# Sample cross-attention of a hybrid decoder step, issued four samples at a time in column groups of the array

## The chip, the cores and the metric

The kernel runs on one core of a Trainium2 chip. The metric is the device time of one execution in microseconds (us). A core has a matrix engine (TensorE, "PE" in the profile, with its weight loads "PEld"), a vector engine (DVE), a scalar engine (ACT), GpSimd (POOL) and a queue engine (SP). They run their own instruction streams and meet at semaphores. Transfers from main memory are issued by SP (weights) and POOL (cached keys and values).

## The reference

One inference step of a two-layer decoder for one prompt of 512 tokens and 8 samples of 4 new tokens each. Both groups share all weights. Every layer is a token mixer, a cross-attention into 256 memory tokens and a SwiGLU block. The change touches the cross-attention of the samples only, in both layers:

```python
def cross_attend(h, mk, mv, wq, wo):
    b, t, _ = h.shape
    q = (h @ wq).reshape(b, t, XATTN_HEADS, XATTN_HEAD_DIM)     # 4 heads of 256
    o, _ = gqa_attend(q, mk, mv, True)
    return o.reshape(b, t, D_MODEL) @ wo
...
        xs = xs + rmsnorm(cross_attend(rmsnorm(xs, gn[2]), cache_mem_k[li], cache_mem_v[li], w_xq[li], w_xo[li]), gn[3])
```

For each sample and head the scores are a 4 x 256 by 256 x 256 product, followed by a softmax over the 256 memory tokens and a 4 x 256 by 256 x 256 product with the values. Each sample has its own keys (1 MB) and its own values (1 MB) per layer, so 32 MB are read for this in all. All of it is float32.

## The kernel before

Activations stand with the channels on the 128 partitions: `x`, `h`, `y` and `mix` hold 8 chunks of 128 channels by 544 tokens (512 of the prompt, then 32 of the samples). `layer_end(l)` runs for both layers: output projection, memory projections, `linear("xq")`, `cross(l)`, `linear("xo")`, and the feed-forward block.

`cross(l)` on TensorE has, in the order of the program:

- `scores(0)`: scores of the first 128 prompt tokens (16 records of 256 columns in the trace, 8 instructions in the program; a float32 matmul leaves two records).
- The scores of the samples. Sample b has its 4 tokens x 4 heads in 16 of 32 columns of a weight tile `xqd[:, b, c, :]`; samples 2q and 2q+1 share the 32 output partitions 32q to 32q+31 of one PSUM bank (the even one fills the first 16, and the other columns are zero). Eight channel chunks c are added up, with the key tile `mk` as the moving operand, 256 columns. The loop is over b, and c is inside.
- `scores(1)`, `turn(0)` (transposes of prompt probabilities), two transposes of the samples' probabilities, then `s_values(0)`: values of samples 0 to 3. Sample j writes output partitions 32j to 32j+31 of two banks f, 512 columns each, adding up two halves kt of the memory tokens. The loop is over j, with f and kt inside.
- `scores(2)`, `turn(1)`, `s_turn(0)`, `scores(3)`, `turn(2)`, `s_values(1)` for samples 4 to 7, `turn(3)`, `s_turn(1)`, and `values()` for the prompt.

Output partitions 32j to 32j+31 belong to columns 32j to 32j+31 of the array. These 32-column strips are called column groups here.

ACT and DVE work between: for each prompt quarter `x_exp` on ACT takes the exponentials and `x_soft` on DVE the maxima and the scaling; `x_evac` on ACT copies the transposes; `s_copy(hb)` copies the value rows of four samples, one bank on each of the two engines, once the count `mv_used` says that the four samples are done.

Key and value tiles of 1 MB come through a ring of 6 places. `TILES` is the order in which POOL loads them; `PLACE` says where tile n goes (n mod 6 here, counted from the layer's first key tile), and `BEFORE` which tile was there. POOL works through the list in order and, ahead of each load, waits until the place's last tile has been used: `mk_used` counts used key tiles and `mv_used` used value tiles. With 8 key tiles and 8 value tiles per layer, key tiles 0 to 5 of the list are loaded well ahead. Key tile 6 takes the place of key tile 0, 7 that of 1, value tile 0 that of key tile 2, value tile 1 that of key tile 3, value tiles 2 and 3 those of key tiles 4 and 5, value tiles 4 and 5 those of key tiles 6 and 7, and value tiles 6 and 7 those of value tiles 0 and 1:

```python
            def tile(n):
                kind, b, kv, hh = TILES[n]
                s = PLACE[n]
                if BEFORE[n] is not None:
                    tile_used(BEFORE[n])
                ...
                else:
                    pool.dma_start(dst, a["mem" + kv][int(kind[3]), b]).then_inc(cfull[s], 16)
```

TensorE waits in `tile_in` for the place's `cache_full` semaphore. The sparse attention earlier in the kernel (L1588 with `to_rows`, `k_scores`, `s_first`) already issues its 32-column matmuls in turn over the four column groups.

Of the kernel before, what the change touches and what calls it, by code (L numbers as in the profile page):

```python
# [34 lines left out]
P = 128  # L35
# [3 lines left out]
NB, NT = 8, 4  # L39
# [125 lines left out]
TILES = [("cmp", b, kv, h) for b in range(NB) for kv in "kv" for h in range(2)]  # L165
for _hb in range(2):
# [4 lines left out]
    if not _hb:  # L171
        TILES += [("win", 1, "k", 0)]
    TILES += [("slc", 4 * _hb + j, "v", h) for h in range(2) for j in range(4)]
TILES += [("mem0", b, kv, 0) for kv in "kv" for b in range(NB)]
TILES += [("mem1", b, kv, 0) for kv in "kv" for b in range(NB)]
TILE = {t: i for i, t in enumerate(TILES)}

XC = 2
# [80 lines left out]
def decoder_step(nc, a, w, o):  # L259

    with ExitStack() as ctx:
# [13 lines left out]
        def S(name):  # L275

            if name not in sems:
                sems[name] = ctx.enter_context(nc.semaphore(name))
            return sems[name]
# [25 lines left out]
        ps = ctx.enter_context(nc.psum_tensor("ps", [P, 8, 512], F32))  # L305
# [66 lines left out]
        xqd = flatx[:, 1280:3328].rearrange("p (b c n) -> p b c n", b=NB, c=8)  # L372
# [69 lines left out]
        def tile_in(e, *t):  # L442

            n = TILE[t]
            e.wait_ge(cfull[PLACE[n]], 16 * TURN[n])
            return place_of(n)
# [71 lines left out]
        def _(pool):  # L518
# [6 lines left out]
            def tile_used(n):  # L525

                kind, b, kv, hh = TILES[n]
                if kind == "cmp":
                    pool.wait_ge(S("sub_ready"), n + 1)
                elif kind == "win":  # L530
                    pool.wait_ge(S("sw_sc" if kv == "k" else "sw_pv"), b + 1)
                elif kind == "slc" and kv == "k":
                    pool.wait_ge(S("kt_tr"), 32 * (b // 4) + 4 * (4 * hh + 3) + b % 4 + 1)
                elif kind == "slc":
                    pool.wait_ge(S("sv_used"), 8 * (b // 4) + 4 * hh + b % 4 + 1)
                else:
                    pool.wait_ge(S("mk_used" if kv == "k" else "mv_used"), 8 * int(kind[3]) + b + 1)

            def tile(n):
                kind, b, kv, hh = TILES[n]  # L540
# [37 lines left out]
            k = 0  # L578
            at = NC
# [1004 lines left out]
        def _(pe):  # L1584
            pe.wait_ge(S("const_loaded"), 32)

            def mm(out, lhsT, rhs, start, stop, **kw):
                return pe.matmul(out, lhsT, rhs, start=start, stop=stop, **kw)  # L1588
# [128 lines left out]
            for u in range(32):  # L1717
                c, g, qt = u // 8, u // 4 % 2, u % 4
# [205 lines left out]
            def cross(l):  # L1924
# [35 lines left out]

                def s_values(hb):

                    for j in range(4):
                        b = 4 * hb + j
                        mv = tile_in(pe, f"mem{l}", b, "v", 0)
                        for f in range(2):
                            for kt in range(2):
                                at = kt * P + 32 * (b // 2)
                                last = mm(ps[32 * j:32 * j + 32, 6 * hb + f, :], xst[:, at:at + 32],
                                          mv[:, kt * 1024 + 512 * f:kt * 1024 + 512 * f + 512], kt == 0, kt == 1)  # L1970
                        last.then_inc(S("mv_used"), 1)

                def s_turn(hb):
                    pe.wait_ge(S("xv_copied_a"), 2 * l + hb + 1)
# [6 lines left out]
                scores(0)  # L1981

                pe.wait_ge(S("xq_apart"), l + 1)
                for b in range(NB):
                    mk = tile_in(pe, f"mem{l}", b, "k", 0)
                    rows = slice(32 * (b // 2), 32 * (b // 2) + 32)
                    for c in range(8):
                        last = mm(ps[rows, 1, 0:256], xqd[:, b, c, :], mk[:, c * 256:c * 256 + 256],
                                  b % 2 == 0 and c == 0, b % 2 == 1 and c == 7)
                    last.then_inc(S("mk_used"), 1)  # L1990
                scores(1)
                turn(0)
                pe.wait_ge(S("xs_norm"), l + 1)
# [195 lines left out]
```

## Time and profile before

| what | value |
|---|---|
| median of 3 runs | 2095.23 us (2095.05 to 2095.54) |
| the profiled execution | 2096.04 us, span 2094.1 us from first to last instruction |
| TensorE busy | 1894.8 us, 90% of the span |
| DVE, ACT, POOL busy | 1001.5, 694.8, 255.8 us |
| memory read | 244.89 MB, 123 GB/s over the span |
| mean granted TensorE clock | 0.954 of full speed |

Nearly all matmuls are recorded on L1588, the helper `mm`; they are told apart by the tiles that they read. In the trace `mc` is the buffer with the ring's places, `big` holds queries and probabilities, `kstore` and `vstore` the prompt's keys and values. `cross(0)` runs from about 636 to 718 us of the span and `cross(1)` from about 1514 to 1598 us. Matmul durations include the way through the array, so that one can start before the one ahead ends; the distance between starts is what a matmul costs.

### The profile page before, as it was taken

The page shows a single profiled execution, that of the slowest core. Times are in us where ns is not written, and L with a number is a line of the kernel's source. Part 1 is how long each engine was busy: PE and PEld are TensorE (multiplying, and loading weights), DVE is VectorE, ACT ScalarE, POOL GpSimd, SP SyncE. Part 2 cuts the span into 40 slices and gives each one's busy share as a digit, 9 for nine tenths or more (in the row PEclk, how much of TensorE's full clock was granted, in tenths as well). Part 3 has the DMA queues.
Part 4 walks back from the last instruction along what each step waited for, and adds up shares of the span by engine and source line. Part 5 has one row for each costly group of instructions (what it writes and reads, how often), then busy time and mean ns, then how long its engine had stood idle before and what let it go on. Part 6 is the DMA issues. An engine that isn't in the chain of part 4 may idle for free.

```text
span 2094.1 us, 31811 instructions
## 1 busy us (share of the span) xinstructions
PE 1894.8 (90%) x13423; PEld 1690.5 (81%) x13423; DVE 1001.5 (48%) x1405; ACT 694.8 (33%) x1155; POOL 255.8 (12%) x231
## 2 busy tenths in 40 slices
PE   5997997669899989999999899798999799999995
PEld 4785664449795679999999799797946799999995
DVE  6994784333642246444422394738322554444223
ACT  2113553344421433222222326545214432222221
POOL 2330001212221021000000112114010300000001
PEclk9997998889999989999999899999999899999998
DMA  6894004762445122222222222335450122222221
GB/s 218 343 372 171 1 1 178 274 268 96 148 164 199 36 67 71 90 82 88 90 84 89 75 71 83 107 137 168 144 201 31 51 91 82 89 90 84 88 85 59
DMA packets 59655, 254.73 MB, mean 122 GB/s; under 512 B 10224, under 2 KB 10624, under 8 KB 45904
## 3 DMA queue, kind: packets, MB, share of 16 engines
q1 hardware_dynamic: 40320, 135.39, 20.1%
q0 software_dynamic: 14656, 109.53, 13.6%
q10 hardware_dynamic: 4576, 8.34, 1.1%
q8 instruction: 77, 1.26, 0.2%
q14 instruction: 26, 0.21, 0.0%
HBM read 244.89 MB, written 12.68 MB: 123 GB/s over the span
## 4 chain that ended last, share of the span: by engine, by line
PE 79%; DVE 12%; ACT 4%; DMA 3%; issue 1%; POOL 0%; SPq 0%; ACTq 0%; POOLq 0%; DVEq 0%
PE ps L1588 75%; DVE work L1107 3%; PE ps L1839 2%; DVE big L1168 1%; PE ps L1756 1%; DVE work_r L1129 1%; DVE rinv L1091 1%; DVE wring_r L1121 1%; ACT whi L679 1%; DMA mc<-in_slck,idx 1%; DVE x L1110 1%; DMA big<-in_slck,idx 1%; ACT work L852 1%; DVE mc L1549 0%; DMA cst<-in_const 0%
## 5 line engine op out<-in xcount | busy, mean ns | idle before, releaser
L1588 PE MATMUL ps<-work_r,whi 128*128 128x272 f32 x4352 | 762.2, 292 | 49.4 <-ACT work_r L691 27.5
L1588 PEld LDWEIGHTS ps<-work_r,whi 128*128 128x128 f32 x4352 | 633.6, 191 | 63.5 <-issue 42.2
L1588 PE MATMUL ps<-work_r,wring_r 128*128 128x272 f32 x2432 | 512.1, 293 | 0.0
L679 ACT ACTIVATE whi<-wring 128x1024 fp32r<-128x1024 f32 (+1 forms) x232 | 242.3, 1045 | 793.2 <-PE ps L1588 791.1
L1121 DVE TENSOR_TENSOR wring_r<-wring,whi 128x1024 fp32r<-128x1024 f32 (+1 forms) x232 | 283.4, 1224 | 439.6 <-ACT whi L679 439.3
L1588 PEld LDWEIGHTS ps<-work_r,wring_r 128*128 128x128 f32 x2432 | 388.6, 193 | 0.0
L1588 PE MATMUL ps<-mc_r,whi 128*128 128x272 f32 x1216 | 242.5, 289 | 0.0
L1588 PE MATMUL ps<-big_r,whi 128*128 128x272 f32 (+1 forms) x960 | 198.1, 293 | 14.0 <-DVE wring_r L1121 14.0
L1588 PEld LDWEIGHTS ps<-mc_r,whi 128*128 128x128 f32 x1216 | 188.5, 189 | 0.0
L1588 PEld LDWEIGHTS ps<-big_r,whi 128*128 128x128 f32 x960 | 155.3, 195 | 15.3 <-DVE wring_r L1121 15.2
L1588 PE MATMUL ps<-mc_r,wring_r 128*128 128x272 f32 x704 | 145.7, 288 | 0.0
L1588 PE MATMUL ps<-work,wring 128*128 128x272 f32 x480 | 119.0, 409 | 6.7 <-DVE work L1098 6.7
L1168 DVE TENSOR_REDUCE big<-mc 128x128 f32<-128x2048 f32 x32 | 115.6, 3680 | 9.7 <-DMA mc<-in_cmpk,idx 7.6
L1588 PEld LDWEIGHTS ps<-work,wring 128*128 128x128 f32 x480 | 95.2, 200 | 27.8 <-issue 7.4
L571 POOL TENSOR_TENSOR ssum<-ssum,sq 128x544 f32<-128x544 f32 (+1 forms) x56 | 78.9, 1409 | 262.7 <-ACT sq L656 260.8
L571 POOL TENSOR_TENSOR ssum<-sq 128x544 f32<-128x544 f32 (+1 forms) x13 | 17.5, 1349 | 758.2 <-ACT sq L656 758.2
L1588 PEld LDWEIGHTS ps<-mc_r,wring_r 128*128 128x128 f32 x704 | 109.9, 189 | 0.0
L1466 DVE TENSOR_TENSOR kstore<-ps,rinv 128x544 f32<-128x544 f32 x44 | 31.9, 724 | 151.1 <-PE ps L1588 151.1
L1588 PE MATMUL ps<-mc,big 128*32 128x256 f32 (+2 forms) x448 | 89.9, 432 | 5.3 <-ACT big L918 5.3
L1461 DVE TENSOR_TENSOR big<-ps,rinv 128x544 f32 (+1 forms) x44 | 31.9, 724 | 112.1 <-PE ps L1588 112.0
L1588 PEld LDWEIGHTS ps<-mc,big 128*32 128x32 f32 x448 | 37.5, 111 | 54.3 <-issue 24.7
L1091 DVE RECIPROCAL rinv<-rms 128x544 f32<-128x544 f32 (+1 forms) x14 | 46.1, 3295 | 27.9 <-ACT rms L668 27.9
(296 smaller groups left out, 2062.8 us busy)
## 6 DMA issues: line engine op xcount, KB each, us to landing
wring<-w_ffn SPq DMA_DIRECT2D x88, 512.0 KB, 3.5
mc<-in_memk POOLq DMA_DIRECT2D x16, 1024.0 KB, 7.5
mc<-in_memv POOLq DMA_DIRECT2D x16, 1024.0 KB, 5.1
wring<-w_down SPq DMA_DIRECT2D x32, 512.0 KB, 3.5
wring<-w_w_out SPq DMA_DIRECT2D x16, 512.0 KB, 4.0
wring<-w_mk SPq DMA_DIRECT2D x16, 512.0 KB, 3.4
wring<-w_mv SPq DMA_DIRECT2D x16, 512.0 KB, 4.1
wring<-w_xq SPq DMA_DIRECT2D x16, 512.0 KB, 3.6
```

The source lines that it names most:

```text
L571: pool.tensor_tensor(ssum[:, 0:wd], sq[:, 0, 0:wd] if c == 1 else ssum[:, 0:wd], sq[:, c % 2, 0:wd], ALU.add).then_inc(S("sq_summed"), 1)
L679: act.activation(dst, src, ACT.Copy).then_inc(S("w_hi"), 1)
L852: act.activation(piece, piece, ACT.Exp, bias=sst[:, 3 * hb + 2, 1:2], scale=SC, accum_out=sxs[:, k:k + 1]).then_inc(S("sx_exp"), 1)
L1091: dve.reciprocal(rinv[:, 0:wd], rms[:, 0:wd]).then_inc(S("rinv_ready"), 1)
L1107: dve.tensor_tensor(y[:, c, :], y[:, c, :], rinv[:, :], ALU.mult).then_inc(S("y_scaled"), 1)
L1110: dve.tensor_tensor(x[:, c - 1, :], x[:, c - 1, :], y[:, c - 1, :], ALU.add).then_inc(S("x_ready1"), 1)
L1121: dve.tensor_tensor(lo, src, F(hi), ALU.subtract).then_inc(S("w_lo"), 1)
L1168: dve.tensor_reduce(subs[:, n % 8, :], src.rearrange("p (r c) -> p c r", r=SUB), AXX, ALU.add).then_inc(S("sub_ready"), 1)
L1461: dve.tensor_tensor(halves(hid[j]), accp[g % 4], halves(rinv[:, :]), ALU.mult).then_inc(drained[g % 4], 1)
L1466: dve.tensor_tensor(halves(uprow[:, j, :]), accp[g % 4], halves(rinv[:, :]), ALU.mult).then_inc(drained[g % 4], 1)
L1588: return pe.matmul(out, lhsT, rhs, start=start, stop=stop, **kw)
L1839: last = pe.transpose(ps[:, j, r * P:r * P + P], kt_[:, at:at + P], ident)
```

## The change

The samples' matmuls of both products are put in another order, and the key tiles are loaded in the order in which they are now used. The matmuls themselves, their number, operands and output places stay the same.

- Scores: first the even samples 0, 2, 4, 6 (`e = 0`), then the odd ones (`e = 1`). Inside each, the loop over chunks c is outside, and the four samples, each in its own column group, follow one another. All four key tiles are waited for ahead of the first matmul, and the four counts of `mk_used` come with the last round, c = 7.
- Values: bank f and half kt are outside, and the four samples follow one another. All four tiles are waited for first, and the four counts of `mv_used` come with the last round.
- `TILES`: key tiles in the order 0, 2, 4, 6, 1, 3, 5, 7 (`MEMK`), and POOL's wait follows it.

```diff
-TILES += [("mem0", b, kv, 0) for kv in "kv" for b in range(NB)]
-TILES += [("mem1", b, kv, 0) for kv in "kv" for b in range(NB)]
+
+MEMK = [2 * q + e for e in range(2) for q in range(4)]
+for _l in range(2):
+    TILES += [(f"mem{_l}", b, "k", 0) for b in MEMK]
+    TILES += [(f"mem{_l}", b, "v", 0) for b in range(NB)]
...
-                    pool.wait_ge(S("mk_used" if kv == "k" else "mv_used"), 8 * int(kind[3]) + b + 1)
+                    at_ = MEMK.index(b) if kv == "k" else b
+                    pool.wait_ge(S("mk_used" if kv == "k" else "mv_used"), 8 * int(kind[3]) + at_ + 1)
...
-                    for j in range(4):
-                        b = 4 * hb + j
-                        mv = tile_in(pe, f"mem{l}", b, "v", 0)
-                        for f in range(2):
-                            for kt in range(2):
-                                at = kt * P + 32 * (b // 2)
+                    mvs = [tile_in(pe, f"mem{l}", 4 * hb + j, "v", 0) for j in range(4)]
+                    for f in range(2):
+                        for kt in range(2):
+                            for j in range(4):
+                                at = kt * P + 32 * ((4 * hb + j) // 2)
                                 last = mm(ps[32 * j:32 * j + 32, 6 * hb + f, :], xst[:, at:at + 32],
-                                          mv[:, kt * 1024 + 512 * f:kt * 1024 + 512 * f + 512], kt == 0, kt == 1)
-                        last.then_inc(S("mv_used"), 1)
+                                          mvs[j][:, kt * 1024 + 512 * f:kt * 1024 + 512 * f + 512], kt == 0, kt == 1)
+                                if f and kt:
+                                    last.then_inc(S("mv_used"), 1)
...
-                for b in range(NB):
-                    mk = tile_in(pe, f"mem{l}", b, "k", 0)
-                    rows = slice(32 * (b // 2), 32 * (b // 2) + 32)
+                for e in range(2):
+                    mks = [tile_in(pe, f"mem{l}", 2 * q + e, "k", 0) for q in range(4)]
                     for c in range(8):
-                        last = mm(ps[rows, 1, 0:256], xqd[:, b, c, :], mk[:, c * 256:c * 256 + 256],
-                                  b % 2 == 0 and c == 0, b % 2 == 1 and c == 7)
-                    last.then_inc(S("mk_used"), 1)
+                        for q in range(4):
+                            last = mm(ps[32 * q:32 * q + 32, 1, 0:256], xqd[:, 2 * q + e, c, :],
+                                      mks[q][:, c * 256:c * 256 + 256], e == 0 and c == 0, e == 1 and c == 7)
+                            if c == 7:
+                                last.then_inc(S("mk_used"), 1)
```

On TensorE, the scores of the samples in `cross(0)` stood so before (`cache_full0` to `cache_full5` are the ring's places, in brackets what an instruction waits for):

```order
L1588 MATMUL ps<-mc,big 32x256 [waits cache_full0,xq_apart]
L1588 MATMUL ps<-mc,big 32x256 x7
L1588 MATMUL ps<-mc,big 32x256 [waits cache_full1]
L1588 MATMUL ps<-mc,big 32x256 x7
...
L1588 MATMUL ps<-mc,big 32x256 [waits cache_full0]
L1588 MATMUL ps<-mc,big 32x256 x7
L1588 MATMUL ps<-mc,big 32x256 [waits cache_full1]
L1588 MATMUL ps<-mc,big 32x256 x7
L1588 MATMUL ps<-kstore,big 128x256 [waits xp_exp]
```

And so they stand now:

```order
L1592 MATMUL ps<-mc,big 32x256 [waits cache_full2,cache_full1,cache_full3,cache_full0,xq_apart]
L1592 MATMUL ps<-mc,big 32x256 x31
L1592 MATMUL ps<-mc,big 32x256 [waits cache_full0,cache_full1,cache_full5,cache_full4]
L1592 MATMUL ps<-mc,big 32x256 x31
L1592 MATMUL ps<-kstore,big 128x256 [waits xp_exp]
```

The second filling of places 0 and 1 was waited for ahead of the seventh and the eighth sample, after 48 and 56 of the 64 matmuls; now both are waited for together after 32 of them.

The first values, `s_values(0)`, on TensorE in `cross(0)` before:

```order
L1588 MATMUL ps<-mc,big 32x512 [waits cache_full2,xs_trc]
L1588 MATMUL ps<-mc,big 32x512 x3
L1588 MATMUL ps<-mc,big 32x512 [waits cache_full3]
L1588 MATMUL ps<-mc,big 32x512 x3
L1588 MATMUL ps<-mc,big 32x512 [waits cache_full4]
L1588 MATMUL ps<-mc,big 32x512 x3
L1588 MATMUL ps<-mc,big 32x512 [waits cache_full5]
L1588 MATMUL ps<-mc,big 32x512 x3
```

And now:

```order
L1592 MATMUL ps<-mc,big 32x512 [waits cache_full4,cache_full3,cache_full5,cache_full2,xs_trc]
L1592 MATMUL ps<-mc,big 32x512 x15
```

The tiles in places 3 to 5 were waited for one after another, between matmuls; now all four are waited for at the start. POOL's list of loads has the same length and the same waits by name.

## Rows read from the trace of the kernel before

**Rows 1.** The page: the chain that ended last, share of the span by engine.
```profile
PE 79%; DVE 12%; ACT 4%; DMA 3%; issue 1%; POOL 0%; SPq 0%; ACTq 0%; POOLq 0%; DVEq 0%
```

**Rows 2.** Chain of work that ended last in cross(0): start, us, what.
```profile
639.88 28.89 PE ps L1588 x144
...
672.53 12.51 PE ps L1588 x48
```

**Rows 3.** Timeline of PE, cross(0): start, us, operation, records [idle before <-releaser].
```profile
639.81 25.31 PE L1588 MATMUL ps<-mc,big 128*32 128x256 f32 x128
665.05 3.72 PE L1588 MATMUL ps<-kstore,big 128*128 128x256 f32 x16
...
672.53 8.86 PE L1588 MATMUL ps<-mc,big 128*32 128x512 f32 x32 [2.67 <-ACT big L918]
681.32 3.72 PE L1588 MATMUL ps<-kstore,big 128*128 128x256 f32 x16
...
693.06 8.86 PE L1588 MATMUL ps<-mc,big 128*32 128x512 f32 x32
```

**Rows 4.** Timeline of PE, the same places in cross(1).
```profile
1518.21 25.31 PE L1588 MATMUL ps<-mc,big 128*32 128x256 f32 x128
...
1550.93 10.53 PE L1588 MATMUL ps<-mc,big 128*32 128x512 f32 x32 [2.67 <-ACT big L918]
1561.39 3.72 PE L1588 MATMUL ps<-kstore,big 128*128 128x256 f32 x16
```

**Rows 5.** Timeline of weight loads: in the first scores, then in s_values(0).
```profile
640.26 3.56 PEld L1588 LDWEIGHTS ps<-mc,big 128*32 128x32 f32 x17
...
673.42 0.11 PEld L1588 LDWEIGHTS ps<-mc,big 128*32 128x32 f32 x1 [0.32 <-issue]
673.85 0.11 PEld L1588 LDWEIGHTS ps<-mc,big 128*32 128x32 f32 x1 [0.32 <-issue]
```

**Rows 6.** Timeline of PE in the sparse attention, matmuls in turn over column groups.
```profile
374.07 0.64 PE L1588 MATMUL ps<-kstore,small 128*32 128x256 f32 x8
374.52 1.04 PE L1588 MATMUL ps<-big,small 128*32 128x512 f32 x8
375.38 0.27 PE L1588 MATMUL ps<-big,work 128*32 128x128 f32 x1
...
378.77 0.27 PE L1588 MATMUL ps<-big,work 128*32 128x128 f32 x1
```

**Rows 7.** Timeline of POOL: first key load of cross(0), and four loads in a row.
```profile
643.75 0.53 POOL L553 DMA_DIRECT2D mc<-in_memk  x1 [54.80 <-PE ps L1588]
...
1354.81 2.18 POOL L553 DMA_DIRECT2D mc<-in_memk  x4 [65.39 <-DVE mc L1563]
```

**Rows 8.** Landing times (us from issue): at 643.7, 1522.1, 1355.4 (second of four), 588.4.
```profile
mc<-in_memk POOLq DMA_DIRECT2D x1, 1024.0 KB, 6.4
mc<-in_memk POOLq DMA_DIRECT2D x1, 1024.0 KB, 5.0
mc<-in_memk POOLq DMA_DIRECT2D x1, 1024.0 KB, 7.1
mc<-in_memk POOLq DMA_DIRECT2D x1, 1024.0 KB, 9.7
```

**Rows 9.** An idle stretch of PE in the timeline; then stretches: us, PE busy (records), granted clock, DMA share, GB/s.
```profile
388.09 0.39 PE L1588 MATMUL ps<-mc,work 128*32 128x128 f32 x1 [8.39 <-DMA mc<-in_slcv,idx]
...
187.00:213.00 26.00, 16.43 (x43) 0.50 0.00 1
388.00:391.00 3.00, 2.91 (x56) 0.50 1.02 429
391.50:393.00 1.50, 1.50 (x64) 1.00 0.28 109
1551.80:1555.00 3.20, 3.20 (x7) 0.50 0.00 0
```

**Rows 10.** Timeline of DVE: scaling of the last prompt quarter's probabilities.
```profile
695.93 1.22 DVE L1415 TENSOR_TENSOR big<-big,small 128x1024 f32<-128x1024 f32 x1
```

## The prediction

> **What bounds the kernel now.** I read four views. The page first: the chain of work that ended last is 79% TensorE [rows 1], so time taken from TensorE is time taken from the kernel wherever nothing else is late. Then that chain in the stretch around the first cross-attention: it goes through the samples' scores without a break (28.89 us over 144 records: 16 of the prompt's and the samples' 128) and, after a step over ACT, through the samples' values [rows 2]. Then the timeline of TensorE for the lengths. The scores run from 639.81 to 665.05, 25.24 us. The values of samples 0 to 3 run from 672.53 to 681.32, 8.79 us [rows 3], and in the second layer from 1550.93 to 1561.39, 10.46 us [rows 4]; the values of samples 4 to 7 are the same 32 records and 8.86 us long [rows 3]. The scores of the second layer have the same 25.31 us [rows 4]. So the reordered matmuls hold TensorE for 25.2 + 8.8 + 8.8 and 25.2 + 10.5 + 8.8 us, 87.3 us in both layers.
>
> **What one matmul costs alone and in turn.** Seventeen weight loads, one for each record, take 3.56 us in the first sample's scores, so the starts are (3.56 - 0.11) / 16 = 0.216 us apart for 256 columns; in the values they are 0.43 us apart for 512 [rows 5]. The sparse attention shows 32-column matmuls that go round the four column groups, with the same types and widths: eight records of 256 columns take 374.52 - 374.07 = 0.45 us, eight of 512 take 0.86 us, and 31 rounds of four records of 128 columns take 378.77 - 375.38 = 3.39 us, 0.109 us for a round [rows 6]. A round of four costs what one record costs alone. I take that: the rotation is worth a factor of four. The Trainium skill (TensorE: Matmul & The Clock Gate, "Why this matters for your kernels") gives 2.38 for three column groups and 3.07 for four row groups, 512 columns each. The trace has a duration for the same thing, and it says 4.0; by 3.07 the sum below would come out about 7 us later.
>
> **Scores, part by part.** The even samples are 64 records, 16 rounds of 0.216 us: 3.46 us. Their four key tiles were loaded long before. Then the program wants four tiles at once for the odd samples, and two of them (samples 5 and 7, places 0 and 1) can't be issued before the even ones are done. This is the new wait. POOL issued its first key load of the stage 643.75 - (639.81 + 3.46) = 0.48 us after the first sample's last record [rows 3, 7]; now the four counts come together at the same 3.46 us, so the issue stays at start + 3.94. The next issue follows 0.55 us later (four in 2.18 us) and the second load of a row landed 7.1 us after its own issue, 7.65 after the first's [rows 7, 8]. A single load took 5.0 us in the second layer and 6.4 in the first [rows 8]; the second comes some 2.6 us behind. So the last tile is there at start + 3.94 + 7.7 = 11.6 us (second layer) and, with the 1.4 us that the first layer's load was longer, some 1.2 us later, 12.8. TensorE idles for about 8 us. Behind it nothing can go: the engine is in order, and scores(1), turn(0) and the values are queued behind the odd samples. The other loads (values 0 and 1) are issued behind the two and don't hold them up.
>
> The odd samples are another 3.46 us at full clock. After the idle 8.39 us at 388.09 the granted clock was 0.50 from before the restart until past 391, and 1.00 by 391.5 [rows 9]. Some 3.4 us at the half level cost 1.7 us: 5.2 us. The scores end at start + 16.8 (layer 1) and + 18.0 (layer 0) instead of + 25.24: a gain of 8.4 + 7.2 = **15.6 us**.
>
> **Wait for values.** From the end of the scores to the first values it is 672.53 - 665.05 = 7.48 us, set by prompt work and ACT's exponentials [rows 3]. That stays. Value tiles 2 and 3 go to the places of key tiles 4 and 5, which are now freed only at the end of the scores. Issued some 0.4 us later, the second lands 7.7 us after that, at 8.1: a wait of 0.6 us in each layer, **-1.2 us**. Tiles 0 and 1 were issued 8 us before, and samples 4 to 7 have 681.32 to 693.06 = 11.7 us for tiles 6 and 7 against 8.1 needed.
>
> **First values.** 8 rounds of 0.43 us: 3.43 us. The idle time ahead of them (2.67 us now) grows to 3.3; after 2.67 us the clock was 1.00 in one layer and 0.50 for 3.2 us in the other [rows 3, 4, 9]. I charge half of that loss, 0.85 us: 4.3 us against 8.79 and 10.46, **10.7 us** gained.
>
> **Second values.** 3.43 us instead of 8.79, but now something else is late. The next instruction on TensorE, turn(3), wants the scaled probabilities of the last prompt quarter, and DVE has them at 695.93 + 1.22 = 697.15, 4.09 us after the values start [rows 3, 10]. So turn(3) starts at + 4.13 instead of + 8.79: 4.66 us in each layer, **9.3 us**. ACT and DVE copy the value rows within 0.7 us of the count, beside turn(3). Copies and prompt values keep their distances.
>
> The other edits cost nothing: POOL issues the same 16 loads per layer, and loading the keys in another order moves bytes but adds none; number and length of weight loads stay. The cover for the loads of keys 5 and 7 was the scores of samples 2 to 5; that cover is gone, and it is priced above.
>
> **Sum.** 15.6 - 1.2 + 10.7 + 9.3 = 34.4 us. From the profiled execution's own 2096.04 us that is 2061.6; the median of the runs is 0.8 us lower, so 2061 us.
>
> **Bounds of the unknown.** The wait for the second key tile: 7.7 us as in an idle queue, or 0.55 + 9.7 = 10.3 us as for two loads that shared the engines with weights [rows 8]; I stay with the first, since no weights are due here. It is worth +4 us over both layers, and the slower first load of layer 0 -1.2. The clock in the odd samples: full, -3.4 us, or half all through (6.9 us), +3.5. The clock in the first values: full -1.7, half all through +5.2. The wait for values: none -1.2. The forecast's own range is thus 2053 to 2069.
>
> **Rivals.**
>
> *Each burst is cold* (20%). The waits fall between short bursts, and the half level might hold from the first idle stretch through all of them. For: the trace has 26 us at 0.50 with 16.43 us of work in it [rows 9], and TensorE would now work some 10 us of the 21 after the even samples. Against: in the sparse attention one restart was enough. Price per layer: 1.7 us in the odd samples are in the sum already; scores(1) and the turns, about 4 us, double, of which 0.6 covers the wait for values: 3.4. The first values take 6.9 instead of 4.3: 2.6. The second take 6.9 instead of 4.13: 2.8. Together 8.8, about 18 in both layers: 2079 us; with the bursts alone cold, 2072. The Trainium skill has this as a rule against such a change (same page, "HAM oscillation — how this bites in real kernels"): short bursts with load waits between them start cold each time. The trace shows it for the burst right behind a long wait.
>
> *The rotation pays less* (5%), because four different key tiles stream at once. Against: in rows 6 four different tiles streamed as well. At a factor of two the even and the odd samples cost 3.46 us more each, the first values 3.43 and the second 6.86 - 4.13 = 2.7: 13 per layer, 2087 us. With no factor at all nothing is gained and the wait is left, so this is also the way in which the change would not do what it says.
>
> *The wait is shorter than I think* (7%). Without any idle time between even and odd samples (8 us and 1.7 us of clock, twice) the time would be 2042 us. Against: a 1 MB tile never landed in under 5.0 us here, and the place must be free first.
>
> *Slower than before* (3%). One mechanism: the long wait takes the clock to the half level and it doesn't come back inside the stage. The forecast gains 17.2 us per layer, so 17.2 us of work done at half clock, 34 us of busy execution beyond what is in the sum, use it up. From the end of the scores to the end of the second values are 693.06 + 8.79 - 665.05 = 36.8 us [rows 3]; less the 2.67 idle and less the 17.6 us of both values, plus 6.9 for the new ones and 3.5 for the odd samples, that is about 27 us of work. If all of it went at half clock, it would lose some 24 us more than I charge, and the kernel would come out at 2061 + 2 x 24 = 2109 us; it turns slower when the half level holds unbroken from the odd samples nearly to the second values in both layers. The longest stretch of this kind here is the 26 us with 16.43 us busy [rows 9], half of what is needed.
>
> **Chances.** The forecast 63%, cold bursts 20%, weaker rotation 5%, shorter wait 7%, slower 3%, no difference 2%. Outside 2050 to 2076 lie most of the slow tail of the cold bursts and of the weak rotation and half of the shorter wait, about 18%. A measurement of this kernel tells about 0.2% (4 us) from no change. All cases but two are far on the fast side: faster 0.95, same 0.02, slower 0.03.
>
> **What the changed kernel's profile would show.** Right: in the timeline 64 sample records in about 3.6 us, an idle stretch of 7 to 10 us put down to a transfer into `mc`, 64 more in 3.5 to 7; the granted clock at 0.5 around it; 32 value records in 3.6 to 5.5 us with an idle stretch a little over 2.67 ahead of them; turn(3) waiting for DVE L1419 (L1415 before) by less than 1 us. Wrong: the first 64 records in more than 4.5 us (rotation), the idle stretch away or over 12 us (loads), a half level that reaches past the first values (clock), or a wait of the prompt's part that I take to keep its distance.

## The result

The changed kernel takes 2061.59 us (median of 4 executions, 2057.45 to 2068.09) against 2095.39 us before (4 executions, 2095.05 to 2096.73): a ratio of 0.9844, 95% interval 0.9822 to 0.9866, 1.6% faster. The forecast was 2061 us. Beside the experiments the same kernel ran twice more, in later batches, and gave 0.9815 (0.9798 to 0.9831) and 0.9837 (0.9806 to 0.9868), 2059.91 and 2061.98 us.

From the page of the changed kernel: its span, the busy times, and the chain that ended last by engine:

```profile
span 2061.5 us, 31823 instructions
PE 1845.8 (90%) x13423; PEld 1672.8 (81%) x13423; DVE 1001.9 (49%) x1405; ACT 694.6 (34%) x1155; POOL 254.8 (12%) x231
PE 77%; DVE 12%; DMA 5%; ACT 4%; issue 1%; POOL 0%; SPq 0%; ACTq 0%; POOLq 0%; DVEq 0%
```

TensorE is busy for 49 us less with the same 13423 records, and the span is only 32.6 us shorter. The other 16 us are idle time in front of transfers, as the timelines below show: twice 7.86 us ahead of the odd samples and twice 0.5 us more ahead of the first values. In the chain, transfers hold 5% instead of 3% [rows 1]. The timeline of TensorE in `cross(0)` (L1592 is L1588 of before), which answers to [rows 3]:

```profile
643.35 3.66 PE L1592 MATMUL ps<-mc,big 128*32 128x256 f32 x64
654.87 5.04 PE L1592 MATMUL ps<-mc,big 128*32 128x256 f32 x64 [7.86 <-DMA mc<-in_memk]
659.84 3.72 PE L1592 MATMUL ps<-kstore,big 128*128 128x256 f32 x16
...
667.78 5.34 PE L1592 MATMUL ps<-mc,big 128*32 128x512 f32 x32 [3.13 <-DMA mc<-in_memv]
673.04 3.72 PE L1592 MATMUL ps<-kstore,big 128*128 128x256 f32 x16
...
684.78 3.64 PE L1592 MATMUL ps<-mc,big 128*32 128x512 f32 x32
688.93 1.09 PE L1949 MATMUL ps<-cst,big 128*128 128x128 f32 x8 [0.52 <-DVE big L1419]
```

And in `cross(1)`, which answers to [rows 4]:

```profile
1503.82 3.66 PE L1592 MATMUL ps<-mc,big 128*32 128x256 f32 x64
1515.34 6.57 PE L1592 MATMUL ps<-mc,big 128*32 128x256 f32 x64 [7.86 <-DMA mc<-in_memk]
1521.85 3.72 PE L1592 MATMUL ps<-kstore,big 128*128 128x256 f32 x16
...
1529.83 3.64 PE L1592 MATMUL ps<-mc,big 128*32 128x512 f32 x32 [3.17 <-DMA mc<-in_memv]
1533.40 3.72 PE L1592 MATMUL ps<-kstore,big 128*128 128x256 f32 x16
```

The rows are read like this. The even samples' 64 records take 3.66 us instead of some 12.6. Then TensorE is idle for 7.86 us, and the releaser (what ended the idle time) is a transfer of keys. The odd samples take 5.04 and 6.57 us for the same number of records, and the difference is the clock, as stretches of the trace show (us, TensorE busy with records, granted clock, DMA share, GB/s):

```profile
655.00:657.50 2.50, 2.50 (x28) 0.50 0.99 419
658.00:660.00 2.00, 2.00 (x37) 1.00 0.46 193
668.00:671.00 3.00, 3.00 (x17) 0.50 1.01 426
1515.50:1521.00 5.50, 5.50 (x56) 0.50 0.73 307
1529.90:1533.00 3.10, 3.10 (x32) 1.00 1.01 423
```

The chain of work that ended last in `cross(0)` (start, us and what) names the whole way of a load between two halves of the samples' scores, and again ahead of the values:

```profile
647.29 0.52 POOL mc L557
647.80 6.93 DMA mc<-in_memk
...
654.87 5.16 PE ps L1592 x64
...
660.18 0.52 POOL mc L557
660.70 6.94 DMA mc<-in_memv
```

The second of two loads issued in a row is the one that is waited for: 0.52 us of POOL's issue of the first, then 6.93 us from its own issue.

### The profile page after: what moved, and what is told of

Its sections match the earlier page's. It is cut to its first block, busy times and chain, and to the rows that moved or that the text cites. A ratio compares the mean times of both kernels' runs of the same rounds, so it can differ in the third digit from the quotient of the medians.

```text
span 2061.5 us, 31823 instructions
## 1 busy us (share of the span) xinstructions
PE 1845.8 (90%) x13423; PEld 1672.8 (81%) x13423; DVE 1001.9 (49%) x1405; ACT 694.6 (34%) x1155; POOL 254.8 (12%) x231
## 4 chain that ended last, share of the span: by engine, by line
PE 77%; DVE 12%; DMA 5%; ACT 4%; issue 1%; POOL 0%; SPq 0%; ACTq 0%; POOLq 0%; DVEq 0%
PE ps L1592 73%; DVE work L1111 3%; PE ps L1843 2%; DVE big L1172 1%; PE ps L1760 1%; DVE work_r L1133 1%; DVE rinv L1095 1%; DVE wring_r L1125 1%; ACT whi L683 1%; DMA mc<-in_slck,idx 1%; DVE x L1114 1%; DMA mc<-in_memv 1%; DMA mc<-in_memk 1%; DMA big<-in_slck,idx 1%; ACT work L856 1%
## 5 line engine op out<-in xcount | busy, mean ns | idle before, releaser
L1592 PE MATMUL ps<-work_r,whi 128*128 128x272 f32 x4352 | 762.7, 293 | 47.8 <-ACT work_r L695 27.5
L1592 PEld LDWEIGHTS ps<-work_r,whi 128*128 128x128 f32 x4352 | 633.7, 191 | 62.0 <-issue 40.9
L1592 PE MATMUL ps<-work_r,wring_r 128*128 128x272 f32 x2432 | 512.8, 293 | 0.0
L1592 PEld LDWEIGHTS ps<-work_r,wring_r 128*128 128x128 f32 x2432 | 388.9, 193 | 0.0
L1592 PE MATMUL ps<-mc_r,whi 128*128 128x272 f32 x1216 | 242.8, 289 | 0.0
L1592 PE MATMUL ps<-big_r,whi 128*128 128x272 f32 (+1 forms) x960 | 198.3, 294 | 13.9 <-DVE wring_r L1125 13.9
L1592 PEld LDWEIGHTS ps<-mc_r,whi 128*128 128x128 f32 x1216 | 188.9, 190 | 0.0
L1592 PEld LDWEIGHTS ps<-big_r,whi 128*128 128x128 f32 x960 | 155.5, 196 | 15.2 <-DVE wring_r L1125 15.1
L1592 PE MATMUL ps<-mc_r,wring_r 128*128 128x272 f32 x704 | 145.9, 289 | 0.0
L1592 PE MATMUL ps<-work,wring 128*128 128x272 f32 x480 | 118.9, 409 | 6.7 <-DVE work L1102 6.7
L1592 PEld LDWEIGHTS ps<-work,wring 128*128 128x128 f32 x480 | 95.4, 200 | 27.6 <-issue 7.4
L1592 PEld LDWEIGHTS ps<-mc_r,wring_r 128*128 128x128 f32 x704 | 110.0, 189 | 0.0
L563 POOL TENSOR_TENSOR x<-x,work 128x544 f32<-128x544 f32 x24 | 43.1, 1795 | 130.1 <-DVE work L1111 130.1
L1111 DVE TENSOR_TENSOR work<-work,rinv 128x544 f32<-128x544 f32 x48 | 58.0, 1240 | 0.2
```

The lines of the kernel that those rows point to most:

```text
L563: pool.tensor_tensor(x[:, c, :], x[:, c, :], y[:, c, :], ALU.add).then_inc(S("x_ready0"), 1)
L1111: dve.tensor_tensor(y[:, c, :], y[:, c, :], rinv[:, :], ALU.mult).then_inc(S("y_scaled"), 1)
```

## The experiments

Eight kernels, and the changed kernel again twice, each with the kernel before on the same chip. The first batch (kernel before 2097.9 us) has keys alone, values alone, load order alone and the changed kernel; the second (2096.2 us) the longer fill, three steps and eight places; the third (2096.2 us) the shorter fill, ten places and the changed kernel. Ratios are to the kernel before of the same batch.

**Keys alone, values alone.** The changed kernel with the old `s_values`, and the kernel before with the new one:

```diff
-                    mvs = [tile_in(pe, f"mem{l}", 4 * hb + j, "v", 0) for j in range(4)]
-                    for f in range(2):
-                        for kt in range(2):
-                            for j in range(4):
+                    for j in range(4):
+                        b = 4 * hb + j
+                        mv = tile_in(pe, f"mem{l}", b, "v", 0)
+                        for f in range(2):
+                            for kt in range(2):
...
```

> Scores of the samples in turn over the column groups with the new load order; the values stay one sample after another. My theory: the scores gain 15 to 17 us over both layers (25.2 us become 3.5 of work, about 8 of waiting for the keys of samples 5 and 7, and 3.5 to 6.6 of work at half or full clock, per layer), less up to 1 us per layer of waiting for value tiles: 2079 to 2082 us. Rival, the wait eats the gain: 2090 or more. Rival, the wait costs less than the trace says because something else was late: under 2072.

> Values of the samples in turn over the column groups; scores and load order as before. My theory: 8.8 to 3.4 us for the first values, 8.8 to 4.1 for the second in each layer (ended by DVE's scaling), 10 us per layer, so 2075 us (2073 to 2078), and together with the keys alone it adds up to the whole change within 3 us. Rival, the two parts hide each other (the value wait that the new score order causes is larger than it looks): the sum of the two parts exceeds the whole by over 5 us.

Measured: keys alone 2078.23 us, 0.9913 (0.9896 to 0.9929), 19.7 us less, a little more than the 2079 to 2082 us expected; values alone 2075.12 us, 0.9889 (0.987 to 0.9909), 22.8 us less. The whole change on the same chip is 38.0 us less, so the parts add up to 4.5 us more than the whole. Each of the three intervals reaches some 3.5 to 4 us to either side, so the medians alone can't tell 4.5 us from nothing. The timeline of keys alone in `cross(0)`:

```profile
638.03 3.66 PE L1592 MATMUL ps<-mc,big 128*32 128x256 f32 x64
649.65 6.14 PE L1592 MATMUL ps<-mc,big 128*32 128x256 f32 x64 [7.96 <-DMA mc<-in_memk]
...
663.21 8.86 PE L1592 MATMUL ps<-mc,big 128*32 128x512 f32 x32 [2.67 <-ACT big L922]
```

and of values alone:

```profile
674.77 3.64 PE L1588 MATMUL ps<-mc,big 128*32 128x512 f32 x32 [2.67 <-ACT big L918]
```

Alone, neither part has the wait for a value tile (the first values wait 2.67 us for ACT in both traces, not 3.13 us for a transfer): with the old value order only the first tile must be there, with the old key order the tiles come early. The traces show two costs that only the whole change has. One is that wait, 0.5 us in each layer. The other is the clock: the first values take 5.26 or 5.27 us instead of 3.57 in four of the six stages in the three traces of the changed kernel, 1.7 us more each, and run at full clock in both layers of both traces here. Together that is about 3.3 us, from few traces. The expectation (parts and whole within 3 us) and its rival (over 5 us) both miss the 4.5 by less than the medians can tell; an interplay of some 3 us is what the traces bear out.

**Load order alone.** The kernel before, values included, with the new load order and the samples' scores in that order, still one sample after another (shown against the changed kernel's scores):

```diff
-                    mks = [tile_in(pe, f"mem{l}", 2 * q + e, "k", 0) for q in range(4)]
-                    for c in range(8):
-                        for q in range(4):
+                    for q in range(4):
+                        b = 2 * q + e
+                        mk = tile_in(pe, f"mem{l}", b, "k", 0)
+                        for c in range(8):
...
```

> Key tiles loaded and used in the order 0, 2, 4, 6, 1, 3, 5, 7, but one sample after another as before. My theory: the order of loads costs and brings nothing, each place is freed after 3.2 us as before, though a step into a new column group now comes at each of the 8 samples instead of each second one and lets the last records of one sample run beside the first of the next: 25.2 us become 20 to 22 per layer if that overlap holds at each step, so 2087 to 2090 us. Rival, only the full rotation overlaps: 2095 us, no change.

Measured: 2090.4 us, 0.9956 (0.994 to 0.9971). It is faster without any rotation. The samples' scores in its timeline:

```profile
640.96 21.98 PE L1592 MATMUL ps<-mc,big 128*32 128x256 f32 x128
662.87 3.72 PE L1592 MATMUL ps<-kstore,big 128*128 128x256 f32 x16
```

21.9 us instead of 25.2 with nothing waiting; twice 3.3 is 6.7 us of the 7.5 measured. 128 records one by one would be 128 x 0.216 = 27.6 us. Before there are 3 steps from one column group to the next, here 7: 2.4 / 3 = 0.80 and 5.7 / 7 = 0.82 us for each step, nearly four records of 0.216. That the next group's matmuls start while some four records of the last group are still to come can be counted at such a step (us, TensorE busy with records, granted clock, DMA share, GB/s), first in the middle of a sample, then at the step from the first sample to the second:

```profile
642.50:643.36 0.86, 0.86 (x5) 1.00 0.00 0
643.58:644.44 0.86, 0.86 (x9) 1.00 0.00 0
```

Four more records lie in the second stretch than in the first. So part of what the change gives comes with any order that steps into another column group at each sample.

**The wait filled with work, twice.** The changed kernel with matmuls ahead of the odd samples' scores, whose output isn't read, first 32 (shown) and then 16:

```diff
                 for e in range(2):
+                    if e:
+                        for i in range(32):
+                            mm(ps[:, 7, 0:256], big[:, i % 8, 0:P], kstore[:, i % 8, :], True, True)
```

> As the changed kernel, with 32 matmuls (64 records of 256 columns, about 7.4 us) put between the even and the odd samples' scores, into a PSUM bank that isn't read; they add nothing to the output. The wait for the keys stays as long, but TensorE is busy in it. My theory (the half clock behind the wait comes from the idle engine): the odd samples cost 3.4 us instead of 4.7 to 6.2 and the first values 3.6 instead of sometimes 5.3, so 3 to 8 us less than the changed kernel in both layers: 2053 to 2058. Rival, the clock isn't what makes the odd samples slow (four loads arriving from memory, or the restart itself): the odd samples stay at 4.7 to 6.2 us and the time at 2061.

Measured: 2067.59 us, 0.9861 (0.9838 to 0.9884). The fill was mis-sized by me: 64 records at 0.216 us are 14 us, not 7.4. Its timeline:

```profile
641.81 14.08 PE L1592 MATMUL ps<-kstore,big 128*128 128x256 f32 x64
655.82 3.66 PE L1592 MATMUL ps<-mc,big 128*32 128x256 f32 x64
```

The fill is 6 us longer than the wait, in each layer, and the time can't be compared; but the odd samples take 3.66 us in both layers, with no wait ahead of them. The other half of the expectation failed: the first values took 5.34 us in both layers, behind 3.21 and 3.33 us of waiting for a value tile.

> As the changed kernel, with 16 matmuls of 256 columns (32 records, 6.9 us) between the even and the odd samples' scores, which add nothing to the output. The fill of 32 was mis-sized: 14.3 us in a wait of 8.2. Now about 1.3 us of idle time are left. My theory (half clock behind the wait comes from the idle time): the gap stays at 8.2 to 8.5 us, the odd samples take 3.3 us instead of 4.7 to 6.2, 2 to 3 us less per layer: 2055 to 2058, or 3 to 6 less than the changed kernel of this batch. Rival, no gain, the work in the wait costs as much as the clock gives back: the same as the changed kernel within 2.

Measured: 2061.32 us, 0.9846 (0.9824 to 0.9867), against 2061.98 of the changed kernel in the same batch: no difference that the medians could tell, where 3 to 6 us were expected. Its timeline in both layers, and the odd samples' stretch in `cross(0)`:

```profile
641.24 7.17 PE L1592 MATMUL ps<-kstore,big 128*128 128x256 f32 x32
649.32 3.66 PE L1592 MATMUL ps<-mc,big 128*32 128x256 f32 x64 [0.91 <-DMA mc<-in_memk]
...
660.94 5.34 PE L1592 MATMUL ps<-mc,big 128*32 128x512 f32 x32 [3.21 <-DMA mc<-in_memv]
...
1510.38 3.66 PE L1592 MATMUL ps<-mc,big 128*32 128x256 f32 x64 [1.07 <-DMA mc<-in_memk]
...
1522.01 5.34 PE L1592 MATMUL ps<-mc,big 128*32 128x512 f32 x32 [3.22 <-DMA mc<-in_memv]
```

```profile
649.40:652.80 3.40, 3.40 (x64) 1.00 1.00 424
```

The keys arrive as late as ever (7.2 us of fill and 0.9 or 1.1 us of wait behind it), and the odd samples cost 3.66 us in both layers instead of 5.04 to 6.57. That the slow odd samples are a matter of the idle engine is shown. Tiles arriving from memory aren't the cause: the transfer engines are as busy here, at a clock of 1.00 (share 1.00, 424 GB/s), as they were in the changed kernel at 0.50 (0.99, 419 GB/s, above). Nor is a restart, of which one is left behind 0.9 or 1.1 us. The gain is in part given back one wait later: the first values took 5.34 us in both layers of this trace. From the first of the samples' scores to turn(3) the profile has 44.4 and 44.6 us, against 46.9 and 45.2 in the changed kernel of the same batch: 2.4 and 0.6 us less, too little for the medians.

**Three steps.** Samples 1 and 3 in the wait, then 5 and 7:

```diff
-                for e in range(2):
-                    mks = [tile_in(pe, f"mem{l}", 2 * q + e, "k", 0) for q in range(4)]
+                for e, qs in ((0, (0, 1, 2, 3)), (1, (0, 1)), (1, (2, 3))):
+                    mks = {q: tile_in(pe, f"mem{l}", 2 * q + e, "k", 0) for q in qs}
...
```

> As the changed kernel, but the odd samples' scores in two steps: samples 1 and 3, whose keys are there, in turn over two column groups while the keys of 5 and 7 arrive, then 5 and 7. Two groups cost 3.46 us for two samples instead of 3.46 for four, but the first step lies in the wait. My theory (the wait is bound by when places 0 and 1 come free and by the load, not by work): the last keys land at the same moment, the scores end 3.46 us behind it instead of 4.7 to 6.2 behind it since the idle stretch is only about 4.8 us and less of the rest runs at half clock; value tiles 2 and 3 are issued 8 us earlier, so the 0.5 us wait ahead of the values goes. 1.7 to 3.5 us per layer less than the changed kernel: 2054 to 2058 us. Rival, the clock falls just as long behind the shorter idle stretch: 2060 to 2062.

Measured: 2059.02 us, 0.9827 (0.9807 to 0.9847), between the expected range and the rival's. Its timeline:

```profile
636.55 7.10 PE L1592 MATMUL ps<-mc,big 128*32 128x256 f32 x96
648.20 6.11 PE L1592 MATMUL ps<-mc,big 128*32 128x256 f32 x32 [4.54 <-DMA mc<-in_memk]
...
661.71 3.64 PE L1592 MATMUL ps<-mc,big 128*32 128x512 f32 x32 [2.66 <-ACT big L922]
```

The last keys come at the same distance from the start (648.20 - 636.55 = 11.65 us; 11.52 in the changed kernel), and the value wait is gone as expected. But my theory of the clock failed: behind 4.54 us of idle time it was lower for as long as behind 7.86, and the last two samples took 6.11 us (6.55 behind 4.49 us in the second layer) where 3.5 were hoped for. The rival holds for that part.

**More places.** Two more places for key tiles, in the half of `work` that no one reads from the end of the query projection to the end of the cross-attention; then two more, in the other half, for value tiles 0 and 1. These are the main lines of the second edit. Beside them, the new places take over semaphores of earlier stages, and with ten places one wait at the kernel's start is merged with another:

```diff
-            s = (n - (TILE[kind, 0, "k", 0] if kind.startswith("mem") else n0)) % (NC + XC)
+            s = (n - n0) % (NC + XC)
+            if kind.startswith("mem"):
+                s = (0, 1, 2, 3, 4, 5, 6, 7, 8, 9, 0, 1, 2, 3, 6, 7)[n - TILE[kind, 0, "k", 0]]
...
+            if s >= NC + XC:
+                at = (ybase, ybase + 2048, 0, 2048)[s - NC - XC]
+                return swork[:, at:at + 2048]
...
                 for n in range(n0 + NC, n0 + 16):
+                    if n == n0 + 6:
+                        acc_done(pool, acc_of(f"xq{l}", 7))
                     tile(n)
```

> As the changed kernel, with two more places for key tiles in a part of the work buffer that lies idle from the end of the query projection to the end of the cross-attention. The keys of samples 5 and 7 are loaded from the end of that projection on, not from the end of the even samples' scores; values 0 to 3 go to the four places that the even samples free. My theory (the wait is one for the place, and nothing else is late behind it): the last key lands about 8 us after the projection, 4.5 us after the start of the scores; 3.3 + 1.3 + 3.5 = 8 us for the scores instead of 16.5 to 18, no wait ahead of the values, full clock through the stage: 10 to 12 us less per layer, 2039 us (2036 to 2044). Rival, the loads collide with the weights of the output projection and the wait is still 4 us or more: 2046 to 2052.

Measured: 2050.81 us, 0.9786 (0.9766 to 0.9806). The wait between even and odd samples, and the one ahead of the first values, in its timeline (the odd samples' rows name two buffers in turn, since two of the tiles lie in `work`), and POOL's issue of the values:

```profile
640.77 3.66 PE L1598 MATMUL ps<-mc,big 128*32 128x256 f32 x64
645.01 0.41 PE L1598 MATMUL ps<-mc,big 128*32 128x256 f32 x2 [0.57 <-DMA work<-in_memk]
...
648.60 3.72 PE L1598 MATMUL ps<-kstore,big 128*128 128x256 f32 x16
...
657.62 5.34 PE L1598 MATMUL ps<-mc,big 128*32 128x512 f32 x32 [4.21 <-DMA mc<-in_memv]
```

```profile
644.71 2.09 POOL L561 DMA_DIRECT2D mc<-in_memv  x4 [7.12 <-PE ps L1598]
```

The scores take 648.60 - 640.77 = 7.8 us instead of 16.5 (8.8 instead of 18.0 in the second layer), about as expected. What I had missed is the next transfer: the scores now end 8.7 us sooner after their start, but the four value tiles can only be issued in a row when the even samples are done, at 644.71, and the fourth is there 12.9 us later, at 657.6. So the wait for values grows from 3.13 to 4.21 us (4.37 in the second layer), and the first values took 5.26 and 5.09 us instead of 3.57, a part of them at half clock. Against the 2.67 us of wait and the full clock that were expected, this is 6.5 of the 12 us that are missing to 2039. Another 2 to 4 us lie outside the stage: from turn(3) of the first layer to the samples' scores of the second this trace has 818.8 us, the others 814.7 to 816.8; why is open, and so is the rest.

> As the kernel with eight places, with two more for value tiles 0 and 1 in the other half of the same buffer, so that they are loaded right behind the keys of samples 5 and 7, and value tiles 2 to 5 take the places of the even samples' keys. With eight places the first values waited 4.2 and 4.4 us instead of 2.7 for tile 3, the fourth of four loads issued together. My theory (four loads in a row take 11 us and two take 7): the last tile lands 4 us earlier, ACT is late again and not the load, the idle stretch is back at 2.7 us: 1.5 to 1.7 us per layer less than with eight places, and up to 1.7 more where the clock stays full: 2044 to 2048 us. Rival, the transfers collide (weights, and keys and values in one row) and the keys come later by what the values gain: 2050 as with eight places.

Measured: 2043.54 us (2042.61 to 2046.95), 0.9754 (0.9735 to 0.9772). POOL's timeline (issues) and TensorE's:

```profile
638.05 1.05 POOL L562 DMA_DIRECT2D work<-in_memk  x2 [46.59 <-PE ps L1599]
639.09 1.05 POOL L562 DMA_DIRECT2D work<-in_memv  x2
646.22 2.08 POOL L562 DMA_DIRECT2D mc<-in_memv  x4 [6.08 <-PE ps L1599]
```

```profile
642.28 3.66 PE L1599 MATMUL ps<-mc,big 128*32 128x256 f32 x64
646.89 0.41 PE L1599 MATMUL ps<-mc,big 128*32 128x256 f32 x2 [0.95 <-DMA work<-in_memk]
...
657.97 0.62 PE L1599 MATMUL ps<-work,big 128*32 128x512 f32 x2 [2.67 <-ACT big L929]
...
661.54 3.72 PE L1599 MATMUL ps<-kstore,big 128*128 128x256 f32 x16
```

The first values wait for ACT again, 2.67 us, and take 661.54 - 657.97 = 3.57 us. In the second layer they wait for ACT too (2.66 us) but take 5.27 us, from 1508.66 to 1513.93, with a stretch of half clock:

```profile
1510.00:1513.00 3.00, 3.00 (x20) 0.50 1.04 431
```

So the wait for the load is gone in both layers, and the clock is not full in both. This is the version that beats both kernels: 52.7 us less than before on the same chip, 18.4 less than the changed kernel.

**The changed kernel again, twice.**

> The changed kernel once more, beside the parts and on the same chip. The four executions so far lie from 2057 to 2068 us, those of before within 2 us. My theory: the spread comes from how long the clock stays at the half level after the 7.9 us waits, 3.5 to 6.9 us for the odd samples' scores in each layer and 3.4 to 6.9 for the first values, up to 14 us together: again 2056 to 2068 with a median near 2061. Rival, the spread is of the transfers and chip: then all four kernels of this batch spread alike.

> The changed kernel on the chip of this batch, as a measure for the other two: 2056 to 2064 us, with the odd samples' scores at 4.6 to 6.2 us.

Measured: 2059.91 us (2056.86 to 2063.78) and 2061.98 us (2054.69 to 2067.32). In the first batch the kernel before ran from 2093.68 to 2099.62 us, so the 2 us that it had shown at first was luck of few runs. In that batch all five kernels spread alike (the changed kernel by 6.9 us, the other four by 5.7 to 7.7), as the rival said. In the third batch the changed kernel spread by 12.6 us and the kernel before by 6.7. Whether a part of the spread belongs to the new waits stays open; the last section names a stretch ahead of them where the clock differs.

## Why the prediction was right

**Rotation.** The step "a round of four costs what one record costs alone" held: 64 records in 3.66 us to the end of the last one are 16 rounds of 0.216 and the tail, and the values' 32 take 3.64 us, or 3.57 from their start to the next start, against 8 rounds of 0.43. The Trainium skill (TensorE: Matmul & The Clock Gate, "Why this matters for your kernels") gives 3.07 for four row groups. With that factor 64 records would take 64 x 0.216 / 3.07 = 4.5 us, an estimate from the page's figure. The trace doesn't agree: here, in float32 and over column groups, a round of four costs one record, a factor of 4.

**Scores.** Forecast 15.6 us, found (25.24 - 16.49) + (25.25 - 18.03) = 16.0 us, from 643.35 to 659.84 and from 1503.82 to 1521.85. The wait was forecast as 8 us and is 7.86. Of its parts one was wrong: the first layer's load was not 1.4 us slower, the second of a row came 6.93 us after its issue there as well, and the last keys were there at start + 11.5 us in both layers. The clock made up for it by chance: 5.0 us for the odd samples in one layer, 6.5 in the other (between starts), where I had 5.2 in both. In the three traces of the changed kernel five of six are 6.07 to 6.51 us and one is 4.97, 6.0 on average. So the half clock costs 2.6 us per layer there and not 1.7: this term was too small, and the other error, the slow load, hid it.

**Wait for values.** Forecast 0.6 us per layer, found 667.78 - 659.84 = 7.94 and 1529.83 - 1521.85 = 7.98 us against 7.48: 0.5.

**First values.** Forecast 10.7 us gained with half a chance of half clock, found 3.5 + 6.9 = 10.4: 5.26 us between starts in `cross(0)`, a part of it at half clock, and 3.57 at full clock in `cross(1)`. One of two is what the forecast charged; in the three traces it is four of six.

**Second values.** Forecast turn(3) at + 4.13, found 688.93 - 684.78 = 4.15, and the releaser is DVE L1419 with 0.52 us, as named.

**Sum.** 16.0 - 1.0 + 10.4 + 9.3 = 34.7 us against 34.4. The profiled execution is 2063.55 us, 32.5 less than the one before; the 2 us between are outside the stage: its first sample scores start 3.54 us later than before (643.35 against 639.81), in work that the change doesn't touch, and 1.5 us come back between the two stages. The closeness of the sum is luck in part. From the first of the samples' scores to turn(3), both layers together, the other two traces of the changed kernel are 31.8 and 33.6 us shorter than the trace of before. The range was narrower than its terms, too: the bounds as listed add up to about 2053.5 and 2074, and the prediction puts the upper end at 2069 without a reason. All twelve executions of the changed kernel lie inside it, from 2054.69 to 2068.09.

**Rivals.** The rotation pays in full. The cold bursts came true in part: each burst behind a wait for a load may run at half clock for a part of its length, but scores(1), the second values and the rest don't; in the stretches above the clock was back within the odd samples or right behind them. The Trainium skill has a rule on bursts between load waits, that each starts cold (same page, "HAM oscillation — how this bites in real kernels"). The traces agree for all ten bursts behind 4.5 to 8.1 us of idle time, and not for the stage as a whole. The shorter wait can't come by itself but can be made, with places: with eight it falls from 7.86 us to 0.57 and 1.56 us, so it was a wait for the place and not for bandwidth. The kernel with ten places comes near the 2042 us of that rival, but a part of its gain is in the wait for values, which the rival left alone.

## What to carry to other kernels

Small matmuls that leave three quarters of the columns empty can be issued in turn over the column groups and run four at a time; but then all their operands are wanted at once, and a ring that fed them one by one is suddenly late with its loads. Count the places that a round holds and the places that are free while it runs, and price what the next round waits for: here more than half of the 18 us of work saved in each layer's scores went back into one wait of 7.9 us and the clock behind it. Where a buffer lies idle for the length of the stage, lend it to the ring, and then look at the next transfer in the row, because it becomes the late one.

## What the runs showed that I had not expected

- TensorE starts matmuls of the next column group while about four records of the last group are still to be done, with no rotation in the program. The prediction took the engine to be strictly in order. It is worth 0.80 to 0.82 us for a step of 256-column records (from the 25.2 and 21.9 us above), and in the values before, (32 x 0.43 - 8.79) / 3 = 1.65 us for 512-column records. An order that changes the group with each sample is worth 7.5 us here by itself.
- The half clock lasted about as long behind 4.5 us of idle time as behind 7.9 us (6.1 and 6.5 us for work of 3.5, and 4.97 to 6.5).
- Half a microsecond of idle time more or less goes with the clock of the first values. Counted over both layers of all twelve traces, they ran partly at half clock in 10 of 12 stages behind 3.13 to 4.37 us of idle time, and in 3 of 12 behind 2.66 or 2.67 us. Behind 0.6 to 1.7 us the odd samples ran at full clock in all six stages, behind 4.5 to 8.1 us partly at half clock in all ten. These are counts; no run changes the idle time ahead of the first values alone.
- The kernel before spreads by more than its first runs told, and so does the time at which the stage starts. The stage's start, ahead of which nothing was changed, lies between 636.55 and 643.35 us in the traces of all the kernels. Part of this is the clock in the sparse attention's preparation, before the changed one in the trace of before and here (us, TensorE busy with records, clock, DMA share, GB/s), first after, then before:

```profile
170.00:218.00 48.00, 33.91 (x166) 0.61 0.22 93
```

```profile
170.00:218.00 48.00, 33.91 (x188) 0.68 0.23 93
```

The same busy time holds 166 records in one and 188 in the other. What decides between them stays open.
